# Expert layer of a decoder trunk: one 0/1 matrix for gather and scatter, gates in the add, output rows scattered in two one-pass parts, second halves keep their rows

## What is computed

```python
logits = (xf @ router_w).astype(jnp.float32)
top_val, top_idx = lax.top_k(logits, TOP_K)            # 2 of 8 experts
gates = jax.nn.softmax(top_val, axis=-1)
...
ys = (silu(x_e @ w_gate[e]) * (x_e @ w_up[e])) @ w_down[e]   # rows of the tokens of expert e
out = zeros.at[token].add(gate * ys)
h = h + rmsnorm(out, ffn_norm_post[i])
```

## Time and profile before

| | us |
|---|---|
| median of 3 runs | 1381.0 (1380.85 to 1382.61) |
| span of the profiled execution, first to last instruction | 1376.2 |
| TensorE busy | 1314.5 (96% of the span) |
| VectorE, ScalarE, GpSimd busy | 668.0, 554.3, 154.0 |
| mean granted TensorE clock | 0.992 of full |
| read from HBM | 383.77 MB |

### The profile page before, as it was taken

How to read it: one execution, slowest core, us unless ns; L and a number is a source line. 1 busy time by engine, 2 the same in 40 slices (tenths; PEclk the granted TensorE clock), 3 DMA queues, 4 the chain that set the end, 5 groups by cost and what they waited for, 6 DMA issues and landing times.

```text
span 1376.2 us, 26638 instructions
## 1 busy us (share of the span) xinstructions
PE 1314.5 (96%) x11493; PEld 1052.2 (76%) x11493; DVE 668.0 (49%) x902; ACT 554.3 (40%) x869; POOL 154.0 (11%) x201
## 2 busy tenths in 40 slices
PE   7999999999998999999999999899999999989995
PEld 7979999888887997998865776577555578657762
DVE  5766644766666565754510762264101066326512
ACT  5467545533336456644411651254000056224401
POOL 6300000000000800000122011203020100220200
PEclk9999999999999999999999999999999999999998
DMA  9307543455554403652799989998999999999895
GB/s 379 126 0 291 199 153 123 143 194 183 183 200 151 154 32 126 258 199 92 276 421 421 420 343 374 420 420 346 366 421 421 420 420 402 362 420 421 338 410 237
DMA packets 55155, 387.56 MB, mean 282 GB/s; under 512 B 6368, under 2 KB 6752, under 8 KB 9216
## 3 DMA queue, kind: packets, MB, share of 16 engines
q1 hardware_dynamic: 54112, 384.07, 70.7%
q10 hardware_dynamic: 432, 1.08, 0.2%
q0 software_dynamic: 496, 0.74, 0.2%
HBM read 383.77 MB, written 2.10 MB: 280 GB/s over the span
## 4 chain that ended last, share of the span: by engine, by line
PE 84%; DMA 6%; DVE 5%; ACT 4%; issue 1%; SPq 0%; ACTq 0%; DVEq 0%
PE banks L2142 21%; PE banks L1893 14%; PE banks L1894 14%; PE banks L1895 14%; PE banks L2068 6%; DMA added<-in_pieces_dram 6%; PE banks L2118 4%; PE banks L2070 3%; PE banks L2103 3%; PE banks L2015 1%; PE banks L2228 1%; PE banks L1917 1%; PE banks L2043 1%; ACT w_high L923 1%; DVE w_low L1371 0%
## 5 line engine op out<-in xcount | busy, mean ns | idle before, releaser
L1371 DVE TENSOR_TENSOR w_low<-raw,w_high 128x2048 fp32r<-128x2048 f32 x93 | 214.4, 2306 | 131.4 <-ACT w_high L923 131.4
L923 ACT ACTIVATE w_high<-raw 128x2048 fp32r<-128x2048 f32 x93 | 178.0, 1915 | 67.7 <-PE banks L2070 65.5
L2142 PE MATMUL banks<-added,token_rows 128*32 128x128 f32 (+2 forms) x3088 | 153.3, 298 | 7.0 <-DMA added<-in_pieces_dram 5.6
L2142 PEld LDWEIGHTS banks<-added,token_rows 128*32 128x32 f32 (+1 forms) x3088 | 115.9, 117 | 48.1 <-issue 19.8
L1893 PE MATMUL banks<-rows,w_high 128*128 128x256 f32 x480 | 136.6, 285 | 2.5 <-DVE rows L1372 2.5
L1893 PE MATMUL banks<-w_high,rows 128*128 128x256 f32 x480 | 137.4, 286 | 0.0
L1894 PE MATMUL banks<-rows,w_high 128*128 128x256 f32 x480 | 135.8, 283 | 0.0
L1895 PE MATMUL banks<-rows,w_low 128*128 128x256 f32 x480 | 135.8, 283 | 0.0
L1895 PE MATMUL banks<-w_high,rows 128*128 128x256 f32 x480 | 135.8, 283 | 0.0
L1894 PE MATMUL banks<-w_low,rows 128*128 128x256 f32 x480 | 135.8, 283 | 0.0
L2068 PE MATMUL banks<-rows,w_high 128*128 128x512 f32 x352 | 124.5, 398 | 1.3 <-DVE rows L1372 1.3
(11 more groups left out here) (252 smaller groups left out, 2355.3 us busy)
## 6 DMA issues: line engine op xcount, KB each, us to landing
raw<-in_pieces_dram SPq DMA_DIRECT2D x195, 1024.0 KB, 7.6
added<-in_pieces_dram SPq DMA_DIRECT2D x162, 1024.0 KB, 17.2
phase<-in_mem_dram SPq DMA_DIRECT2D x2, 1024.0 KB, 6.9
early<-in_constants_dram SPq DMA_DIRECT2D x1, 1088.0 KB, 14.1
h_res<-in_x_dram SPq DMA_DIRECT2D x2, 512.0 KB, 4.4
phase<-in_mix_norm_post_dram SPq DMA_DIRECT2D x2, 512.0 KB, 4.4
phase<-in_xa_norm_post_dram SPq DMA_DIRECT2D x2, 512.0 KB, 6.5
kept<-h_res SPq DMA_DIRECT2D x2, 512.0 KB, 11.1
```

Source lines behind the costliest of these rows:

```text
L923: return act.activation(out_, in_, ACT.Copy, scale=scale)
L1371: return dve.tensor_tensor(out_, in_, plain(high), ALU.subtract)
L2142: return pe.matmul(dst, stay, move, start=start, stop=stop, skip_group_check=True)
```

## The change

- Gather and scatter of a unit use one matrix, `places_of[e % 2]`, with ones in place of the gates and with the repeated slots; GpSimd writes it in ten instructions for units 1 to 9, once the scatter of unit e-2 is done. Unit 0's matrix is written by VectorE as before, and its repeats are added by GpSimd after the first gather.
- The gates go into `add_share`: VectorE multiplies the bank by the token's gate in the instruction that adds it.
- Output rows are taken in two float32r parts: ScalarE writes the high part of each 512 columns, VectorE then subtracts it from the bank to get the low part, in the order of column halves. `share` multiplies the 0/1 `spread` by the high and the low part, two one-pass matmuls for one float32 matmul, and it waits for each column half by itself, with the halves in the order 0, 2, 1, 3.
- Units 3 and 8 are of the same expert as units 1 and 6 and of the same parity, so their gathers, copies, `rows_high` and `rows_low` are left out; the rows stay in `token_rows`.
- Class 3 is compiled for units 1, 3, 6 and 8 alone.

```diff
+WIDE_UNITS = tuple(u for u in range(COUNT_UNITS) if STRAIGHT[u] == 3)
...
+def rows_kept(u):
+
+    return u >= 2 and UNITS[u][0] == UNITS[u - 2][0]
+
+
+ROW_SETS = [sum(not rows_kept(i) for i in range(u + 1)) for u in range(COUNT_UNITS)]
+
+
+def share_order(u):
+
+    return (0, 2, 1, 3) if u + 1 < COUNT_UNITS else (0, 1, 2, 3)
+
+
...
-        place_g = view(after_heads, 3072, TT, SEQ)
-        spread = view(after_heads, 3584, 2, SEQ)
+        y_parts = view(after_parts, 0, 2, D)
+        places_of = (place, view(after_parts, 3072, TT, SEQ))
...
-        def halves_of_output(dst, blocks):
-
-            if blocks == 1:
-                return [(dst[:, 0, j * HALF:(j + 1) * HALF], banks[:, j, :]) for j in range(2)]
-            return [(dst[:, j, :], banks[:, 2 * j:2 * j + 2, :].rearrange("p a b -> p (a b)")) for j in range(2)]
+        def output_in_parts(e, groups):
+
+            return blocks_of(groups) == 1 or e in WIDE_UNITS
+
+        def output_parts(blocks):
+
+            parts = []
+            for hh in range(2):
+                at = slice(hh * HALF, (hh + 1) * HALF)
+                for m in range(blocks):
+                    low_at = y_parts[:, 1, at] if blocks == 1 else piece_high[:, m, at]
+                    parts.append((banks[:, 2 * m + hh, :], y_parts[:, m, at], low_at, 2 // blocks))
+            return parts
+
+        def output_block(j):
+
+            return y_sb[:, j, :], banks[:, 2 * j:2 * j + 2, :].rearrange("p a b -> p (a b)")
...
-            def gated_places(e):
-                n = UNITS[e][0]
-                pool.wait_ge(spread_full, e)
+            def repeats(t, place_of, n):
+                for i, again in enumerate(rank_again):
+                    slots = slice((i + 1) * QUARTER, (i + 2) * QUARTER)
+                    ins = pool.tensor_scalar(place_of[:, t, slots], iota[:, slots], again[:, t, n:n + 1],
+                                             chosen[:, t, n:n + 1], ALU.is_equal, ALU.mult)
+                return ins
+
+            def places(e):
+                n, place_of = UNITS[e][0], places_of[e % 2]
+                if e >= 2:
+                    pool.wait_ge(spread_full, e - 1)
                 for t in range(TT):
-                    g = gate[:, t, n:n + 1]
                     for slots in (slice(0, QUARTER), slice(P, SEQ)):
-                        pool.tensor_scalar(place_g[:, t, slots], iota[:, slots], rank[:, t, n:n + 1], g, ALU.is_equal, ALU.mult)
-                    for i, again in enumerate(rank_again):
-                        slots = slice((i + 1) * QUARTER, (i + 2) * QUARTER)
-                        ins = pool.tensor_scalar(place_g[:, t, slots], iota[:, slots], again[:, t, n:n + 1], g,
-                                                 ALU.is_equal, ALU.mult)
-                    ins.then_inc(place_g_ready, 1)
-
-            def places(e):
-                n = UNITS[e][0]
-                pool.wait_ge(gathered, ROW_PAIRS * e)
-                for t in range(TT):
-                    pool.tensor_scalar(place[:, t, :], iota, rank[:, t, n:n + 1], chosen[:, t, n:n + 1],
-                                       ALU.is_equal, ALU.mult).then_inc(place_ready, 1)
+                        pool.tensor_scalar(place_of[:, t, slots], iota[:, slots], rank[:, t, n:n + 1], chosen[:, t, n:n + 1],
+                                           ALU.is_equal, ALU.mult)
+                    repeats(t, place_of, n).then_inc(place_ready, 1)
 
             pool.wait_ge(rank_ready, 2)
-            for e in range(COUNT_UNITS):
-                if e + 1 < COUNT_UNITS:
-                    places(e + 1)
-                gated_places(e)
+            places(1)
+            pool.wait_ge(gathered, ROW_PAIRS)
+            for t in range(TT):
+                ins = repeats(t, places_of[0], UNITS[0][0])
+            ins.then_inc(repeats_ready, 1)
+            for e in range(2, COUNT_UNITS):
+                places(e)
...
-                    move(*halves_of_output(y_sb, blocks)[0]).then_inc(y_first, 1)
+                    if output_in_parts(e, groups):
+                        for src, high, _, count in output_parts(blocks):
+                            move(high, src).then_inc(y_high, count)
+                    else:
+                        move(*output_block(0)).then_inc(y_high, 4)
...
-                    if e == 0:
-                        act.wait_ge(x_by_dve, len(FIRST_BY_DVE))
-                        act.wait_ge(x_ready, len(FIRST_BY_ACT))
+                    if rows_kept(e):
+                        act.nop().then_inc(rows_high_ready, 1)
                     else:
-                        act.wait_ge(x_ready, ROW_PAIRS * (e + 1))
-                    move(rows_high[:, :, :], token_rows[:, e % 2, :, 0:P]).then_inc(rows_high_ready, 1)
+                        act.wait_ge(x_ready, ROW_PAIRS * ROW_SETS[e])
+                        move(rows_high[:, :, :], token_rows[:, e % 2, :, 0:P]).then_inc(rows_high_ready, 1)
...
-            def add_share(e, i):
-
-                t, hh = i // 2, i % 2
-                dve.wait_ge(sum_full, e * 4 + (i + 1))
-                dst = res[:, t, hh * HALF:(hh + 1) * HALF]
+            def add_share(e, nth):
+
+                i = share_order(e)[nth]
+                t, hh, n = i // 2, i % 2, UNITS[e][0]
+                dve.wait_ge(sum_full, e * 4 + (nth + 1))
+                dst, of_token = res[:, t, hh * HALF:(hh + 1) * HALF], gate[:, t, n:n + 1]
                 if e == 0:
-                    move(dst, banks[:, i, :]).then_inc(sum_added, 1)
+                    move(dst, banks[:, i, :], of_token).then_inc(sum_added, 1)
                 else:
-                    dve.tensor_tensor(dst, banks[:, i, :], dst, ALU.add).then_inc(sum_added, 1)
+                    dve.scalar_tensor_tensor(out=dst, in0=banks[:, i, :], scalar=of_token, in1=dst, op0=ALU.mult,
+                                             op1=ALU.add).then_inc(sum_added, 1)
...
-                    move(*halves_of_output(y_sb, blocks)[1]).then_inc(y_second, 1)
+                    if output_in_parts(e, groups):
+                        taken = 4 * e
+                        for src, high, low_at, count in output_parts(blocks):
+                            taken += count
+                            dve.wait_ge(y_high, taken)
+                            low(low_at, src, high).then_inc(y_done, count)
+                    else:
+                        dve.wait_ge(y_high, 4 * (e + 1))
+                        move(*output_block(1)).then_inc(y_done, 4)
...
-            def share(e, halves):
+            def share(e, nths):
 
                 pe.wait_ge(spread_ready, e + 1)
-                pe.wait_ge(y_first, e + 1)
-                pe.wait_ge(y_second, e + 1)
-
-                def add(blocks):
-                    for i in halves:
+
+                def add(blocks, in_parts):
+                    for nth in nths:
+                        i = share_order(e)[nth]
                         t, hh = i // 2, i % 2
-                        for m in range(blocks):
-                            ins = pe.matmul(banks[:, i, :], spread[:, m, t * P:(t + 1) * P],
-                                            y_sb[:, m, hh * HALF:(hh + 1) * HALF], start=(m == 0), stop=(m == blocks - 1))
+                        at = slice(hh * HALF, (hh + 1) * HALF)
+                        pe.wait_ge(y_done, 4 * e + 2 * (hh + 1) if in_parts else 4 * (e + 1))
+                        to = [spread[:, m, t * P:(t + 1) * P] for m in range(blocks)]
+                        if not in_parts:
+                            terms = [(plain(to[m]), y_sb[:, m, at]) for m in range(blocks)]
+                        elif blocks == 1:
+                            terms = [(to[0], y_parts[:, 0, at]), (to[0], y_parts[:, 1, at])]
+                        else:
+                            terms = [(to[m], part[:, m, at]) for m in range(blocks) for part in (y_parts, piece_high)]
+                        for k, (stay, rows_of) in enumerate(terms):
+                            ins = pe.matmul(banks[:, i, :], stay, rows_of, start=(k == 0), stop=(k == len(terms) - 1))
                         ins.then_inc(sum_full, 1)
 
                 with pe.If(counts["pe"][e] < P + 1):
-                    add(1)
+                    add(1, True)
                 with pe.Else():
-                    add(2)
+                    add(2, e in WIDE_UNITS)
...
-                    pe.wait_ge(place_g_ready, TT * (e + 1))
+                    if e:
+                        pe.wait_ge(place_ready, TT * (e + 1))
+                    else:
+                        pe.wait_ge(repeats_ready, 1)
+                    place_of = plain(places_of[e % 2])
```

More of the change, by code:

```diff
@@ L69, with classes_of @@
 MOST = {0: QUARTER, 1: HALF_BLOCK, 2: P, **WIDE_SLOTS}
+WIDE_UNITS = tuple(u for u in range(COUNT_UNITS) if STRAIGHT[u] == 3)
+assert 0 not in WIDE_UNITS and all(u + 1 not in WIDE_UNITS for u in WIDE_UNITS)
+def rows_kept(u):
[3 more added lines that the diff above has]
```

(18 more changed lines are left out.)

21 lines of the change are left out of this document (10 added, 11 removed).

## The result

The changed kernel takes 1370.9 us (median of 4 runs, 1368.6 to 1371.1); the kernel before takes 1380.9 beside it (1378.9 to 1382.6). The ratio is 0.9929, 95% interval 0.9913 to 0.9944. Forecast were 1370 us in a range of 1364.5 to 1377, so the size is met.

The account below looks back on a forecast made before the run. The prediction took the weight stream to bound the expert layer, TensorE counting only around four stalls. Gains of 11.8 less losses of 0.7 and 0.3 gave 10.8 us: 1381.0 - 10.8 = 1370.2, predicted as 1370, range 1364.5 to 1377.

Parts of the forecast that it names:

- The rule: Expert layer: TensorE time saved ahead of or in a weight-stream stall counts in full; where the stream is saturated, nothing.
- The price of the shares: Output shares at 0.232 us per one-pass matmul: 1.58 us saved per light unit, 3.55 per wide unit.
- the term of 3.55: Wide unit 3's share, standing in unit 4 inside the second stall: its whole saving of 3.55 us counts.
- the four stretches: Second part of each wide unit and what follows: stream at 335, 331, 367, 341 GB/s, losing 34.9 us in all.
- The sum of 10.8: Whole kernel: 11.8 us gained by shares, less 0.7 at unit 1's first product and 0.3 in the tail.
- 0.5 and 0.4: Shares of units 1 and 6, in units 2 and 7: gains taken where 1.1 and 1.3 us of stall remained.
- The losses: Output in two parts: unit 1's first product 0.7 us later, share starts 0 to 1 taken as 0, tail 0.3.
- The tail: End of the layer: high and low parts taken one after another, 0 to 0.5 us later, 0.3 lost.
- The gathers at 0: Eight gathers dropped in units 2 and 7, 7.5 us of TensorE behind a full stream: worth 0.
- The one matrix and the gates at 0: Fewer GpSimd instructions per unit, with 13 us of cover, and VectorE's multiply-add in place of an add: each worth 0.
- The clock: Rival: longer waits before units 3 and 8 lower TensorE's clock, making the kernel slower, 1384 us; chance 0.06.
- The rival's 14 us: Clock rival's loss: 14 us from low clock at the start of each second half, giving 1384; chance 0.06.

Follow-up runs that it names:

- e5: Changed kernel with one of the three one-pass products of each half piece left out in the wide units; 1348.7 us, ratio 0.9767.
- c4: Changed kernel plus transposes ahead of weight waits and VectorE's own second high part, with the gathers of units 3 and 8 made again; 1367.4 us.
- e1: Changed kernel, but units 3 and 8 gather and split their rows again; 1372.1 us, ratio 0.9942.
- c3: Changed kernel plus transposes ahead of weight waits and VectorE's own second high part, with unit 3's share in float32; 1368.7 us.
- e3: Changed kernel with the share of unit 3 alone in float32; 1371.8 us, ratio 0.9946.
- e4: Changed kernel with the shares of units 1, 4 and 6 in float32; 1373.4 us, ratio 0.9957.
- e7: Changed kernel, but in light units VectorE takes the second high part itself in place of ScalarE; 1369.1 us, ratio 0.9906.
- e2: Changed kernel with all units' output rows and shares in float32 as before; one matrix, gates in the add and kept rows stay; 1383.0 us.
- c2: Changed kernel plus transposes ahead of the waits for weights and VectorE's own second high part in light units; 1367.7 us, ratio 0.9907.

## Why the prediction was right, point by point

**The rule.** TensorE's time counts only in or ahead of a stall: shown by e5 (22.2 us gained, 26.2 of stall there, at most 1.8 us left in any of them), by c4 (4.2 and 3.2 us more work at the ends of units 2 and 7, no longer time) and by e1 (layer 677.7 us against 677.8).

**The price of the shares.** Light: 0.93 us for four records, 0.232 each, as predicted. Wide: 2.11 in place of 3.63 us, so about 3.1 us a unit and not 3.55. The one-pass records of a wide share begin with one that takes longer; TensorE's timeline of the changed kernel:

```profile
835.87 0.50 PE L2178 MATMUL banks<-after_parts 128*128 128x512 f32 x1 [0.20 <-DVE piece_high L1409]
836.21 0.40 PE L2178 MATMUL banks<-piece_high,after_parts 128*128 128x512 f32 x1
836.44 0.39 PE L2178 MATMUL banks<-after_parts 128*128 128x512 f32 x1
```

The second starts 0.34 us behind the first, the third 0.23 behind the second. The prediction took the pace inside a long run of such matmuls. A wide share stands between float32 records, and its run of eight has its ends; the light share in unit 1 follows products of its own form and has no such start. So the rate was right, the term of 3.55 was 0.45 too large. By an estimate from the figure of about 131 ns that the Trainium skill gives ("TensorE: Matmul & The Clock Gate", "Back-to-back issue gap") a wide unit would have saved 16 x 0.10 = 1.6 us more; no run here shows that pace.

**Where they count.** The stalls one by one, in us, by the four stretches; "again" is the profiled execution of the changed kernel measured again, with 346, 374, 396 and 375 GB/s:

| stall | before | predicted gain | gain, first | gain, again |
|---|---|---|---|---|
| first | 10.2 | 1.58 + 0.5 - 0.7 = 1.4 | 1.1 | 1.3 |
| second | 10.7 | 1.58 + 3.55 = 5.1 | 2.6 | 5.1 |
| third | 6.4 | 1.58 + 0.4 = 2.0 | 3.0 | 3.4 |
| fourth | 7.6 | 1.58 + 0.7 = 2.3 | 2.1 | 3.2 |

The sum of 10.8 lies between the traces' 8.8 and 13.0, and the times say 10.1 and 11.3. The fixed stretches count somewhat too much, because the units move ahead and the start of the fourth stall leaves its stretch (1200:1290 runs at 418 and 416 GB/s in place of 421): the last weights land 7.2 and, measured again, 1357.96 - 1346.99 = 11.0 us earlier. The terms did less well than the sum, and that the sum came out is in part luck. The second stall gave its 5.1 only where the clock held up in unit 3, and not for the reason counted: unit 3's share is worth 2.4 to 2.6 there (c3, e3), so some 0.9 of the 5.1 has another source, which no run shows. The third gave more than predicted, and here a step failed: the shares of units 1 and 6 were capped by what remained of the stall from 830 and from 1180 on, 1.1 and 1.3 us, and then halved to 0.5 and 0.4; e4 shows 1.4 us for each, of which up to 0.45 is its own longer wait (0.65 in place of 0.20). For unit 6 the third stall agrees; a cap read off a fixed stretch of the trace was too tight, and halving it had no row behind it. For unit 1 the first stall gave no more than predicted. A term that the prediction didn't have may have taken the rest: TensorE began the layer about 2 us later in both executions of the changed kernel. Why, and how much of it counts, stays open. Too little in unit 6, and by e4 in unit 1, and 0.45 to 1 too much in unit 3 nearly cancelled.

**The losses.** First product of unit 1: predicted 0.7 later, measured 5.04 - 4.39 = 0.65. That ScalarE's extra move sets it is half the story: e7 shows that VectorE's extra subtraction would do so in its place. The share's wait for the low parts at the start of unit 2 is 0.20 us (the row above), within its bounds of 0 and 1. The tail: predicted 0.3 later, measured 12.10 - 11.86 = 0.24 at the last VectorE instruction; the end of the span, some 6 us behind it, moves by 0.1 in one execution (18.2 against 18.3 us) and by 0.4 in the other (1365.6 - 1346.99 = 18.6).

**The gathers at 0**: shown by c4 and by e1's layer. The reason given was misread, though: the 26.0 and 27.3 us that the prediction calls waits are the lengths of transfers, from issue to landing. TensorE worked through most of them, as this stretch of before shows, which is the 26.0 us at the end of unit 2:

```profile
866.40:892.40 26.00, 20.43 (x277) 11.67 (x277) 7.83 (x11) 6.98 (x10) 7.57 (x12) 0.93 1.02 421
```

It was idle for 5.6 us, not 26. The term is 0 because TensorE waited there at all, so that work dropped ahead of it only lengthens the wait. **The one matrix and the gates at 0**: neither was undone by itself. e2, which keeps both, is no faster than before, so no gain of theirs shows; more isn't known.

**The clock.** It fell in a small way, inside what the range had allowed for it. Before, unit 8 started at 1.2 GHz, and so it did with the gathers back (e1), so that fall isn't the change's; in the first execution of the changed kernel units 3 and 8 both did (stretch 850:940 at 0.94), in the second only unit 8:

```profile
892.46 1.08 PE banks L2201 x32
...
894.89 0.23 PE banks L1947
...
1231.49 1.94 PE banks L2201 x32
```

The waits ahead of units 3 and 8 did grow, by 5.5 and 7.2 us of idle time. The rival's 14 us did not come, because in these rows the clock is back before the wide unit is far in: the sixth product of unit 3 ends 896.71 + 0.43 - 892.35 = 4.79 us behind the unit's start in the first execution, and 894.89 + 0.23 - 892.46 = 2.66 us in the second, so about 2.1 us were lost. The Trainium skill's rule that activity releases the throttle ("TensorE: Matmul & The Clock Gate", "What's actually happening") agrees with the five executions with transposes, where work without use kept both starts at 1.08 us.

**From span to time.** The prediction let the median stand 4.8 us above the span. In all twelve runs of the experiments an execution's own time is 1.7 to 1.9 us above its span; by that, the profiled execution of before was itself some 3 us shorter than the median. It did no harm, since the sum was taken off the median. But the two spans alone, 1376.2 and 1369.0, would have given 7.2 us for a change of 10; some 2 us of the difference lies ahead of the layer.

## What to carry to other kernels

Where a transfer stream and an engine take turns as the bound, count an engine's saved time only in the stretches where the stream falls below its full rate; busy shares of 94 to 96% say little, since 41 us less busy time (1287.8 to 1246.5, e5) brought 22 us. A saving next to the end of a stall should be priced at its full size with a range, not capped by a fixed stretch of one trace, because the stall moves with the change. And work dropped where an engine waits is worth nothing. It may even cost something if the idle engine's clock falls: without the transposes unit 3 started at 1.2 GHz in three of the seven executions that drop the gathers and in neither of the two that keep them, which is too few to show it. Two traces are compared best from the point on where the change begins, since the work ahead of it differed by up to 5.4 us between executions here.

## What the runs showed of the hardware

- TensorE's clock at the start of a unit differs between executions of the same kernel: 1.93 and 1.08 us for the same 32 records at the start of unit 3. Transposes without any use, put ahead of the waits, kept it at full speed there (unit 8 at 1.08 in five executions of five with them, at 1.93 or 1.94 in nine of nine without). In c2's execution it was low at the start of unit 6 instead (0.91 in the stretch 1090:1110), where no transposes stand.
- A stream of one-pass float32r matmuls of 512 columns goes at 0.23 us each, but a run of eight between other work takes 2.04 to 2.11 us, 0.26 each; a run of four behind products of the same form takes 0.93.
- Two profiled executions of the same kernel differed by 3.4 us (spans 1369.0 and 1365.6; layers 681.3 and 677.8), and the gains in single stalls by up to 2.5: a term of that size needs more than one trace.
